# A hybrid SSD, dilated attention and short convolution layer: loads of the merge issued in the stage before, first splits of the output inside the merge, the scan's y copied out in two halves

## The reference

```python
h = rms_norm(x, norm_pre)
proj = h @ w_in                      # z, xbc, dt, q, k, v, g_attn, u, b, c, g_sc, merge
y_ssm = ssd_branch(z, xbc, dt_raw, ...)                       # 16 chunks of 128 tokens, a state between them
y_attn = attention_branch(q, k, v) * silu(g_attn)             # 3 dilated windows, weighed by their lse
y_sc = b_sc * causal_depthwise_conv(c_sc * u, sc_conv_w) * silu(g_sc)
gates = sigmoid(merge).reshape(b, s, 3, D_MODEL)
merged = gates[0] * (y_ssm @ p_ssm) + gates[1] * (y_attn @ p_attn) + gates[2] * (y_sc @ p_sc)
out = merged @ w_out
return x + rms_norm(out, norm_post)
```

## Time and profile before

| | |
|---|---|
| median of 3 runs | 2938.43 us (2933.14 to 2949.33) |
| the profiled execution | 2936.59 us, its span 2935.0 us |
| TensorE busy | 2812.6 us, 96% of the span |
| VectorE, ScalarE, GpSimd busy | 54%, 42%, 54% |
| mean granted TensorE clock | 0.985 |
| DMA | 436.06 MB, mean 149 GB/s |

### The profile page before, as it was taken

One profiled execution on the slowest core, in us unless ns is written; L12 is line 12 of the kernel. 1 busy time (PEld: TensorE's weight loads), 2 busy tenths in 40 slices (PEclk: granted clock), 3 DMA queues, 4 the chain that ended last, 5 costly groups with the idle time before them and its releaser, 6 DMA issues. The chain is left out here.

```text
span 2935.0 us, 40526 instructions
## 1 busy us (share of the span) xinstructions
PE 2812.6 (96%) x14222; PEld 2374.6 (81%) x14222; DVE 1592.8 (54%) x2525; ACT 1238.8 (42%) x2242; POOL 1587.0 (54%) x1078
## 2 busy tenths in 40 slices
PE   6999999999999999999999999998999988899898
PEld 5788888888877888888877888887999966688787
DVE  6335235896534447865335555555667685653433
ACT  5232234333234443332325555555666653432332
POOL 7678778777767788777754454543111253332000
PEclk8999999999999999999999999999999999999999
DMA  4657336432235455322346464646555377855443
GB/s 122 152 152 240 114 115 170 126 112 87 72 94 172 131 155 133 106 89 72 94 136 181 135 186 143 182 144 214 160 164 156 119 240 234 276 182 172 157 150 107
DMA packets 462803, 436.06 MB, mean 149 GB/s; under 512 B 60737, under 2 KB 403009, under 8 KB 454977
## 3 DMA queue, kind: packets, MB, share of 16 engines
q1 hardware_dynamic: 457904, 416.87, 47.9%
q10 hardware_dynamic: 2448, 8.91, 0.8%
q0 software_dynamic: 2304, 8.39, 0.7%
HBM read 290.99 MB, written 143.13 MB: 148 GB/s over the span
## 5 line engine op out<-in xcount | busy, mean ns | idle before, releaser
L531 PE MATMUL p_acc<-h_kept,w_hi 128*128 128x512 f32 x1216 | 477.4, 393 | 4.8 <-DVE p_stage L737 3.1
L533 PE MATMUL p_acc<-h_kept,w_lo 128*128 128x512 f32 x1216 | 475.5, 391 | 0.0
L532 PE MATMUL p_acc<-h_kept,w_hi 128*128 128x512 f32 x1216 | 474.2, 390 | 0.0
L417 POOL TENSOR_TENSOR w_lo<-p_sums,w_hi 128x512 fp32r<-128x512 f32 x300 | 391.5, 1321 | 134.8 <-ACT w_hi L618 134.8
L618 ACT ACTIVATE w_hi<-p_sums 128x512 fp32r<-128x512 f32 x300 | 189.2, 632 | 477.0 <-PE p_acc L533 451.2
L531 PEld LDWEIGHTS p_acc<-h_kept,w_hi 128*128 128x128 f32 x1216 | 228.8, 188 | 54.3 <-ACT work L577 3.3
L533 PEld LDWEIGHTS p_acc<-h_kept,w_lo 128*128 128x128 f32 x1216 | 228.8, 188 | 49.8
L532 PEld LDWEIGHTS p_acc<-h_kept,w_hi 128*128 128x128 f32 x1216 | 228.9, 188 | 48.7
L531 PE MATMUL p_acc<-p_ops,w_hi 128*128 128x512 f32 x608 | 241.2, 397 | 7.1 <-DVE p_ops L719 7.1
L533 PE MATMUL p_acc<-p_ops,w_lo 128*128 128x512 f32 x608 | 239.0, 393 | 0.0
L532 PE MATMUL p_acc<-p_ops,w_hi 128*128 128x512 f32 x608 | 237.3, 390 | 0.0
(11 more groups left out here) (337 smaller groups left out, 6793.1 us busy)
## 6 DMA issues: line engine op xcount, KB each, us to landing
raw<-w_in SPq DMA_DIRECT2D x100, 512.0 KB, 5.2
p_rawb<-w_in SPq DMA_DIRECT2D x76, 512.0 KB, 5.2
s_qs<-p_stage SPq DMA_DIRECT2D x96, 256.0 KB, 4.0
work<-s_gates SPq DMA_DIRECT2D x48, 512.0 KB, 7.7
s_xbc<-p_stage SPq DMA_DIRECT2D x32, 512.0 KB, 2.6
work<-s_xbc SPq DMA_DIRECT2D x16, 1024.0 KB, 7.0
spare<-s_qs SPq DMA_DIRECT2D x16, 1024.0 KB, 5.4
att_all<-s_att SPq DMA_DIRECT2D x24, 528.0 KB, 5.2
```

The costliest lines, as they stand in the source:

```text
L417: tt(w_lo[:, k], weight(u, k), w_hi[:, k], ALU.subtract).then_inc(w_made, 1)
L531: pe.matmul(bank, hi, ops[k][:, 0, c], start=c == 0, stop=False)
L532: pe.matmul(bank, hi, ops[k][:, 1, c], start=False, stop=False)
L533: last = pe.matmul(bank, lo, ops[k][:, 0, c], start=False, stop=c == 3)
```

## The change

- **Scan.** `y_out` moves to a buffer `keep` that outlives the stage. TensorE signals `out_made` after each four of the eight turns, ScalarE copies y in two halves of 512 columns, the turns of B wait for the first half and the products of B and C for the second. The final wait for y's store is left out; the attention waits for it before it first loads y.
- **Attention.** The eight loads of y_ssm are spread over pairs 0 and 1, the first weights go to pair 2. Behind the four stores of window 1 of the last pair, SP issues `load_ahead`: the four chunks of y_sc into `work`, and unit 1's weights; then comes the last store.
- **Merge.** No load goes through ScalarE's queue any more. The shares of the attention of unit 8 are made in unit 7 (`weigh` is parted from `add_windows`). In unit 11 SP loads y_ssm, y_sc and y_attn of the second half, each as soon as its lane is free. Two more chunks of w_out are loaded. After its last gates ScalarE makes the high parts of the output's first tile and of w_out's chunks 0 to 2, VectorE their low parts. The attention lane of unit 19 is left for the output stage.
- **Output.** VectorE first does that lane's product and sum (it then goes to HBM by SP), then the low parts from chunk 3 on. The load of tile 1 is issued before the last chunk of w_out; in the loop the load of tile c+2 follows the load of x for tile c. Its PSUM is the merge's.

```diff
@@ scan, SP, TensorE, ScalarE
-                        sp.wait_ge(out_taken, c + 2)
+                        sp.wait_ge(out_taken, 2 * c + 4)
...
-                sp.wait_ge(stored, 16 * TILES + 16)
                 for j in range(2):
                     sp.wait_ge(g_stored[j], 16 * UNITS + 16)
...
-                        pe.wait_ge(out_taken, c + 1)
+                        pe.wait_ge(out_taken, 2 * c + 1)
                         for g in range(GROUPS):
                             last = pe.transpose(ps_m[:, g * P:(g + 1) * P], b_t[:, g], ident[:])
                         last.then_inc(b_transposed, 1)
+                        pe.wait_ge(out_taken, 2 * c + 2)
...
-                        act.wait_ge(out_made, c + 1)
                         act.wait_ge(stored, 16 * c + 16)
-                        act.activation(y_out[:], ps_m[:].rearrange("p (b t) -> p b t", t=P), ACT.Copy
-                                       ).then_inc(out_taken, 1)
+                        for half in range(2):
+                            at = slice(4 * half, 4 * half + 4)
+                            act.wait_ge(out_made, 2 * c + half + 1)
+                            act.activation(y_out[:, at], ps_m[:].rearrange("p (b t) -> p b t", t=P)[:, at], ACT.Copy
+                                           ).then_inc(out_taken, 1)
@@ attention, SP
+                def load_ahead():
+                    sp.wait_ge(v_turned, NV * PAIRS)
+                    sp.wait_ge(v_ordered, FIRST * PAIRS)
+                    sp.wait_ge(k_made, 2 * PAIRS + FIRST)
+                    for c in range(4):
+                        sp.dma_start(first_sc(work, c), d["y_sc"][c, :, :HALF]).then_inc(handed["sc_loaded"], 16)
+                    sp.wait_ge(handed["w"], 1)
+                    load_weights_of(sp, w, raw, 1, (0, 1), handed["raw_loaded"])
+
                 load_q(0, 0, 0, 2)
-                load_first_block(sp, w, d, raw, y_lo, next_loaded)
...
                     if i + 1 < PAIRS:
                         load_k(i + 1, 0, 2 * i + 2)
+                        if i == 0:
+                            sp.wait_ge(first["y_out"], 16 * TILES + 16)
+                        load_first_block(sp, w, d, raw, y_lo, next_loaded, i)
                     for g in range(3):
                         if i + 1 < PAIRS:
                             load_q(i + 1, 0, 2 * i + 2, g)
+                        elif g == 2:
+                            load_ahead()
                         store(i, g)
@@ merge, SP
-                load_weights(0, 1)
...
+                        if u == 0:
+                            sp.wait_ge(y0_made, FIRST_SC + lane + 1)
...
+                    if u == SECOND - 1:
+                        sp.wait_ge(acc_made[0], SECOND - 2)
+                        load_y(0)
...
                     elif u == SECOND - 1:
-                        sp.wait_ge(turned, pair + 2)
-                        for c in range(AHEAD):
-                            sp.dma_start(y_ahead[c], d["y_ssm"][c, :, HALF:]).then_inc(ahead_loaded, 16)
+                        sp.wait_ge(acc_made[1], SECOND - 2)
+                        load_y(1)
+                        sp.wait_ge(acc_made[2], SECOND - FULL)
+                        sp.wait_ge(y_stored, 16 * 4 + 16)
+                        load_y(2)
@@ merge, ScalarE
-                load_y(1, 0)
-                hi_of_y(0, 0, 1)
+                for c in range(FIRST_Y, SSM_N):
+                    copy(y_hi[c], y_raw[c]).then_inc(y_hi_made, 1)
                 for u in range(SECOND):
+                    split(u + 1, (u + 1) % 2, chunks_of(u + 1), [raw_count(u + 1, part) for part in range(2)])
                     if u == 0:
-                        hi_of_y(1, 0)
-                    split(u + 1, (u + 1) % 2, chunks_of(u + 1), [raw_count(u + 1, part) for part in range(2)])
-                    if u < LATE or u >= FULL:
-                        weights_of_windows(u if u < LATE else u - LATE)
+                        act.wait_ge(handed["sc_loaded"], 64)
+                        for c in sc_raw:
+                            copy(y_hi[c], sc_raw[c]).then_inc(y_hi_made, 1)
+                    if u < LATE or u > FULL:
+                        shares_of_windows(u if u < LATE else u - LATE)
+                        scale_windows(u if u < LATE else u - LATE)
+                    elif u == FULL - 1:
+                        shares_of_windows(LATE)
                     gates(u, lanes(u, u % 2))
+                    if u == FULL - 1:
+                        scale_windows(LATE)
...
+                act.wait_ge(out_ahead[0], 16)
+                act.wait_ge(acc_made[0], UNITS - 2)
+                copy(m_hi[:, 0], m_raw[0]).then_inc(parts["m_hi"], 1)
+                for c in range(W_SPLIT):
+                    act.wait_ge(out_ahead[1 + c], 16)
+                    copy(ow_hi[c], ow_raw[c]).then_inc(parts["w_hi"], 1)
@@ merge, VectorE
                     if u == SECOND - 1:
-                        lo_of_y(range(6), 12, y1_made)
+                        lo_of_y(range(SSM_N), 12, y1_made)
                     if u >= FULL:
                         gate_lane(2, use_of(2, u))
...
+                second_unit(NM // 2 - 1, 0)
+                u = UNITS - 1
+                gate_lane(0, use_of(0, u))
+                dve.wait_ge(parts["m_hi"], 1)
+                tt(m_lo[:, 0], m_raw[0], m_hi[:, 0].bitcast(F32), ALU.subtract).then_inc(parts["m"], 1)
+                lo_of_w(0)
+                gate_lane(1, use_of(1, u))
+                add_first(use_of(1, u), 1, UNITS // 2 - 1)
+                for c in range(1, W_SPLIT):
+                    lo_of_w(c)
@@ output, SP
                 for c in range(W_AHEAD, KC):
+                    if c == KC - 1:
+                        load_m(1, 1)
+                        sp.wait_ge(last_summed, 2)
                     sp.dma_start(w_raw[c], w["w_out"][0, c * P:(c + 1) * P, :]).then_inc(w_loaded[c], 16)
+                sp.dma_start(d["merged"][KC - 1, :, HALF:], total_odd[:]).then_inc(total_stored[1], 16)
...
-                        load_m(2 * i + k + 1, 1 - k)
                         load_x(2 * i + k, k)
+                        load_m(2 * i + k + 2, k)
@@ output, ScalarE and VectorE
-                hi(0, 0, 0)
-                for c in range(KC):
+                for c in range(W_SPLIT, KC):
...
-                lo(0, 0)
-                for c in range(KC):
+                dve.tensor_tensor(last_gate, b_acc[:, 2], last_gate, ALU.mult).then_inc(last_summed, 1)
+                dve.wait_ge(last_summed, 1)
+                dve.tensor_tensor(total_odd[:], total_odd[:], last_gate, ALU.add).then_inc(last_summed, 1)
+                for c in range(W_SPLIT, KC):
```

More of the change, by code:

```diff
@@ L1334, in _, with load_first_block, load_weights_of, first_sc @@
                         last.then_inc(yn_made, 1)
-def load_first_block(sp, w, d, raw, y_lo, loaded):
-    for c in range(8):
-        sp.dma_start(y_lo[c].bitcast(F32), d["y_ssm"][c, :, :HALF]).then_inc(loaded, 16)
+def load_first_block(sp, w, d, raw, y_lo, loaded, part):
+    if part < 2:
+        for c in range(4 * part, 4 * part + 4):
+            sp.dma_start(y_lo[c].bitcast(F32), d["y_ssm"][c, :, :HALF]).then_inc(loaded, 16)
+        return
     for p, at, n in (("p_ssm", 0, 8), ("p_sc", 8, 4)):
         sp.dma_start(raw[:, at:at + n], w[p][0, :, :P].rearrange("(c p) n -> p c n", p=P)).then_inc(loaded, 16)
-FIRST_Y, FIRST_W, W_AHEAD = 4, 12, 3
+def load_weights_of(sp, w, raw, m, branches, loaded):
+    for br in branches:
+        _, p, at, n = BRANCHES[br]
+        sp.dma_start(raw[:, at:at + n], w[p][0, :, m * P:(m + 1) * P].rearrange("(c p) n -> p c n", p=P)
+                     ).then_inc(loaded[at > 0], 16)
+def first_sc(work, c):
+    return work[:].rearrange("p k t -> p (k t)")[:, c * HALF:(c + 1) * HALF]
+FIRST_Y, FIRST_W, W_AHEAD, W_SPLIT = 4, 12, 5, 3
 N_ATT, N_GT = 2 * 3 * (SLOTS // 2) * (PAIR + 4), KV // P * 2 * P
@@ L1758, in merge_branches_stage @@
         y_raw = [lo.bitcast(F32) for lo in y_lo]
-        y_ahead = [att_all[:, c * HALF:(c + 1) * HALF] for c in range(AHEAD)]
+        sc_raw = {FIRST_SC + c: first_sc(work, c) for c in range(4)}
+        ow_hi, ow_raw, m_raw, m_hi, m_lo = output_buffers(raw, work, spare, split_keys, att_all)
         att_loaded, g_loaded, low_made, ex_made, step, ex_scaled, part_made, part2_made, o_half, o_made, ya_hi_made = (
@@ L1832, in load_gate, with load_y @@
                                                            ].rearrange("o p t -> p (o t)")).then_inc(gate_loaded[lane], 16)
+                def load_y(br):
+                    y, _, at, n = BRANCHES[br]
+                    for c in range(n):
+                        sp.dma_start(y_raw[at + c], d[y][c, :, HALF:]).then_inc(y_loaded[(at + c) // 2], 16)
                 def total_of(m, half):
@@ L1908, in second_half @@
                             load_weights(SECOND, u + 2)
+                        elif k:
+                            sp.wait_ge(w_made, UNITS)
```

(12 more changed lines are left out.)

142 lines of the change are left out of this document (72 added, 70 removed).

## The result

The changed kernel takes 2904.64 us (median of 4 runs, 2894.62 to 2911.98), the kernel before 2938.44 beside it (2933.14 to 2949.33): ratio 0.9879, 95% interval 0.9843 to 0.9915. The forecast was 2904. Its parts are less good than their sum. The profiled execution, at 2911.98, was the slowest of the four; its span is 2910.1.

A forecast was written before the change was run, and what follows sets the result against it. TensorE, busy 96% of the span, was taken as the bound, so only its idle time and low-clock passes could go. Terms -4.5 -1.4 -5.1 -1 -2.9 -11 -7 = -32.9 gave 2904 us, range 2889 to 2920.

The forecast's parts named there:

- third rival: Unit 0, unit 12, output and scan: waits move instead of going; -15.9 with the rest unchanged, 2920 us; chance 0.20.
- Scan, halves: Scan: copying y in halves removes TensorE's 0.3 us wait in 15 chunks; -4.5 us, bounds -4.8 and +2.9.
- Scan to attention: Attention's start: SP no longer waits for y's store, the last gate store is late next; -1.4 us.
- First K: Attention's start: K of unit 1 leaves 5 us earlier and ScalarE's wait goes; -5.1 us, bounds -6.5 and 0.
- Merge, unit 0: Merge's start: y_sc wait goes, but the last store lands behind six loads; turn -1 us, bounds -6 and +3.5.
- A barrier before the merge that comes over 4 us later: Before merge unit 0: a sign of being wrong; the forecast had the barrier 1 to 2 us later.
- The rival in which the queue lets the store past: Second rival, merge unit 0 (or GpSimd's early split, unit 8): 4 to 9 us better, 2896 us; chance 0.14.
- Merge, unit 8: Turn of unit 8: shares made a unit earlier, GpSimd late next; -2.9 us, bounds -1 and -7.6.
- Merge, unit 12: Before unit 12: the 12.36 us stop goes, some 3 us given back; -11 us, bounds -14.4 and -6.
- Start within 2 us of unit 11's end: Merge: expected sign that unit 12 starts within 2 us of unit 11's end, with small stops in it.
- Output: Output's start to second tile: early splits and VectorE's last sum off TensorE's path; -7 us, bounds -8.8 and -5.
- slower rival: Scan: the extra ScalarE instruction, repeated 16 times, comes late in each chunk; 2953 us, chance 0.02.

The follow-up runs named there:

- run 2: Kernel before, with only the ten merge loads moved from the attention's start to pairs 0 to 2: 2933.15 us, ratio 0.9982.
- runs 4 and 5: Changed kernel: in 4 the last store issued before the six merge loads, 2902.85 us; in 5 those loads issued two stores earlier, 2893.22 us.
- run 6: Changed kernel, with the shares of unit 8's attention made in unit 8 again: 2904.96 us, ratio 0.9897.
- run 8: Changed kernel, with the last unit's attention lane multiplied and added inside the merge again: 2909.06 us, ratio 0.991.

## Why the prediction was right, and where it was not

**The sum: partly luck.** The median fell by 33.8 and 32.9 was forecast. But the interval of the ratio is over 20 us wide, and in the two profiles the stretches that the change touches give -29.1: the scan missed its term by 6.9, and the parts behind it gave 31.5 where 28.4 was forecast. Some figures in the prediction are wrong as well. Its own bounds add up to -49.5 and -5.6 (2887 and 2931), not -50.6 and -8.1; its third rival adds up to -18.9, not -15.9 (2918 to 2920). The loads ahead of K were 5.0 MB in the unit used elsewhere, not 4.7. None of these touches the 2904.

**Scan, halves: the term that was mis-sized.** "So the 0.3 us wait goes in 15 chunks: -4.8" is true, and was taken for a gain in time. Behind the wait stands the mask product, which waits for ScalarE's s_fall and VectorE's s_mix. TensorE came to it 0.54 earlier in each chunk and it began only 0.23 earlier; it waited 7.2 to 10.0 in the five profiles with whole copies, 8.4 in the mean, and 9.9 to 13.2 in seven with halves, 11.9 in the mean. The forecast had even said that the turn of B starts the chain to the next mask, and had not priced what follows. So some -3.5 by the trace, for -4.5. The larger miss was not in the forecast at all: the changed kernel's profile has one long stop for s_yn (3.7, with the clock down in two chunks), and its scan is 8.0 longer than the mean of the four with halves and no long stop. That makes +2.4 for -4.5.

**Scan to attention** came out at -1.4 as forecast, with the gate store next: it landed at 2015.5 and ScalarE began the attention's first split at 2016.1, before y's store landed at 2016.8. That it is right to the tenth is luck: over all profiles the gap is 6.6 to 6.8 without the edit and 5.4 to 6.1 with it.

**First K.** The mechanism held (run 2 alone: -6.8). The size, -7.3, lies beyond the bound of -6.5: ScalarE's wait was taken as the price, and TensorE's recovery after the stop was in it too (six passes in 1.51 us for 0.85 in their like later), and a later stop of the attention shrank from 1.43 to 0.92.

**Merge, unit 0.** The order in SP's queue held: landed at 2348.0 for 2349 foreseen. The barrier was missized: 1 to 2 us later was foreseen, it was 4.3, since six issues held SP for 7.8 and not 5 (p_sc alone 3.10). "A barrier before the merge that comes over 4 us later" stood among the prediction's own signs of being wrong, and it came. The turn came out at -2.0 because the weighing took 8.7 from its first step to the turn and not 10. The rival in which the queue lets the store past is refuted by runs 4 and 5 together: the store lands in 10.8 with the six loads ahead of it, in 7.9 with them behind, in 6.3 with none of them near. What neither forecast nor rival had was that the place was free: two stores earlier is worth another 7.

**Merge, unit 8.** GpSimd is late next, as said, with a stop of 3.48 where 4 to 5 was named (1.4 to 3.8 in seven other profiles with the edit); -3.9 for -2.9, of which the shares are 2.3 (run 6).

**Merge, unit 12.** -10.1 for -11, but by other stops. "Start within 2 us of unit 11's end" failed: unit 13's weights hold SP for 7.6, and ScalarE makes its first two high parts together at 2543.42, 6.92 after it was free, as two chunks share one semaphore. "Small stops in it" failed too: after its start TensorE never waits over 0.5 (in the profiles of runs 5 and 6, which started 1.8 and 1.9 late, one stop of 1.36 and one of 1.16 came). The 3 to be given back were paid ahead of the unit, 3.88, not in it.

**Output.** -6.8 for -7: barrier 0.91 for 1.2, chunk 7 1.06 for 1, the second tile 0.88 for 1, and no low clock, for which 1 was kept, as the three stops of about 1 us here did not make it fall (1.00 from 2723 to 2740).

The third rival, waits that move, was right in part for the scan and for nothing else. The slower rival did not show: in the scan TensorE never waited for either half of the copy.

## What to carry to other kernels

A wait of TensorE is worth what is left when the chain behind it is followed to its next wait: here 4.8 us of copy waits went, the mask waits grew by 3.5 in the mean, and some 3.5 us were gained. A load issued early is only early enough when it stands ahead of every store that a barrier or a reader waits for, and its cost there is SP's time to issue it (up to 4.6 us for one in the changed kernel, 8.15 before) as much as its bytes: the same six loads cost 4.3 at the barrier in one place and nothing two stores earlier. And before an edit of a few us is judged by medians, look in the profiles for what scatters the executions; one or two stops of 3 to 8 us that come and go hide it.

## What the runs showed of the hardware

- One DMA issue held SP for 0.3 to 0.6 us where little was in flight, and for 3.10, 4.62 and 8.15 us (p_sc, 256 KB) behind loads already issued.
- VectorE's four-instruction s_yn, 1.67 us alone, took 2.45 to 2.49 when GpSimd's cast (1.04 to 1.25) began 0.93 to 1.18 us into it, and 4.5 to 4.6 when the cast began within 0.7 us and the subtraction (2.40) met it as well.
- After six of nine stops of 2.8 to 3.7 us in the scan the eight turns behind them took 1.80 to 1.97 us, after three 1.09. Stops of 0.9 to 1.1 at the output's start left the granted clock at 1.00 (2.4 GHz); one of 3.5 (run 8) was followed by 0.50 (1.2 GHz).
- A store of 1056 KB landed 6.3, 7.9 or 10.8 us after its issue, by what stood in the queue with it.
